# Rearranging the first stage, the way into block two, and the way out of its attention

## The reference

```python
# block one
proj = x @ w_in + b_in                      # 22 tiles of 256 columns; f (the forget gate) first
y_a = hgrn2_mixer(q, f, i, g) @ w_proj_a    # chunked linear attention, 4 heads
y_b = moba_mixer(mq, mk, mv) @ w_proj_b     # softmax attention, 8 heads of 64
mixed = (sigmoid(gate_a) * y_a + sigmoid(gate_b) * y_b) @ w_out
x = layer_norm(ALPHA * x + mixed)
x = layer_norm(ALPHA * x + hier_moe(x))     # 32 experts, top 2
# block two, on 16 meta tokens + 256 tokens (L = 272)
h = concat(meta, x)
h = h + pool_mixer(rmsnorm(h), pool_w)      # windows 2, 4, 8, 16; then 4 blocks of 256x256
h = h + swiglu(rmsnorm(h), gate, up, down)  # 1024 -> 2816 -> 1024
h = h + sb_mixer(rmsnorm(h))                # stick-breaking attention, 16 heads
h = h + swiglu(rmsnorm(h), gate, up, down)
out = rmsnorm(h)[16:]
```

## Time and profile before

| what | us |
|---|---|
| median of 3 runs | 1244.81 (1243.44 to 1244.97) |
| the profiled execution: its own time | 1242.74 |
| its span | 1241.4 |
| TensorE matmul busy | 1095.2 (88%) |
| VectorE / ScalarE / GpSimd busy | 584.9 / 476.6 / 96.9 |
| mean granted TensorE clock | 0.946 of full |
| DMA | 329.84 MB, 266 GB/s on average |
| chain that ended last | PE 59%, DMA 31%, VectorE 3% |

### The profile page before, as it was taken

How to read it: one execution, slowest core, us unless ns; L and a number is a source line. 1 busy time by engine, 2 the same in 40 slices (tenths; PEclk the granted TensorE clock), 3 DMA queues, 4 the chain that set the end, 5 groups by cost and what they waited for, 6 DMA issues and landing times.

```text
span 1241.4 us, 22394 instructions
## 1 busy us (share of the span) xinstructions
PE 1095.2 (88%) x9774; PEld 913.4 (74%) x9774; DVE 584.9 (47%) x859; ACT 476.6 (38%) x634; POOL 96.9 (8%) x94
## 2 busy tenths in 40 slices
PE   8999999998666767666676999999999998999998
PEld 7999889864232323232333999999999998999997
DVE  5765657633212222212112766664554556666643
ACT  6544763132111111111123644433357764444432
POOL 1540000000000000000000210000110007000011
PEclk9999999999897878888878899999999999999999
DMA  9943547999999999999999746545534245565530
GB/s 336 303 148 116 187 150 300 422 419 420 422 421 420 421 421 421 420 421 420 412 421 403 251 155 201 188 153 171 186 114 142 86 128 178 170 203 164 178 101 35
DMA packets 144689, 329.84 MB, mean 266 GB/s; under 512 B 5507, under 2 KB 115388, under 8 KB 119886
## 3 DMA queue, kind: packets, MB, share of 16 engines
q1 hardware_dynamic: 142528, 321.99, 68.8%
q10 hardware_dynamic: 1470, 4.29, 1.0%
q0 software_dynamic: 592, 2.10, 0.5%
HBM read 327.30 MB, written 1.06 MB: 264 GB/s over the span
## 4 chain that ended last, share of the span: by engine, by line
PE 59%; DMA 31%; DVE 3%; ACT 2%; POOL 2%; issue 2%; SPq 0%; DVEq 0%; ACTq 0%; POOLq 0%
PE PS L444 14%; PE PS L445 14%; PE PS L446 14%; DMA half<-in_w_down_dram 9%; DMA spare<-in_w_down_dram 8%; DMA raw<-in_w_down_dram 7%; DMA half<-in_w_gate_up_dram 5%; PE PS L779 3%; DMA spare<-in_w_gate_up_dram 2%; PE PS L454 1%; PE PS L455 1%; PE PS L456 1%; PE PS L520 1%; PE PS L765 1%; ACT hi L1308 1%
## 5 line engine op out<-in xcount | busy, mean ns | idle before, releaser
L1788 DVE TENSOR_TENSOR lo<-raw,hi 128x2048 fp32r<-128x2048 f32 (+1 forms) x112 | 252.4, 2258 | 143.3 <-ACT hi L1308 112.1
L1308 ACT CAST hi<-raw 128x2048 fp32r<-128x2048 f32 (+1 forms) x113 | 209.5, 1858 | 101.1 <-PE PS L446 90.3
L444 PE MATMUL PS<-AH,hi 128*128 128x272 f32 (+1 forms) x832 | 238.1, 286 | 1.3 <-DVE AL L2273 1.3
L446 PE MATMUL PS<-AH,lo 128*128 128x272 f32 (+1 forms) x832 | 237.6, 286 | 0.0
L445 PE MATMUL PS<-AL,hi 128*128 128x272 f32 (+1 forms) x832 | 237.3, 285 | 0.0
L444 PEld LDWEIGHTS PS<-AH,hi 128*128 128x128 f32 x832 | 157.4, 189 | 2.2 <-issue 1.2
L446 PEld LDWEIGHTS PS<-AH,lo 128*128 128x128 f32 x832 | 157.3, 189 | 0.0
L445 PEld LDWEIGHTS PS<-AL,hi 128*128 128x128 f32 x832 | 156.9, 189 | 0.1
L2204 DVE TENSOR_TENSOR Y<-PS,Y 32x256 fp32r<-32x256 f32 x128 | 53.9, 421 | 131.4 <-ACT Y L1513 128.5
L2195 DVE TENSOR_TENSOR T<-T,PS 64x256 f32<-64x256 f32 x32 | 13.5, 423 | 193.1 <-ACT T L1505 193.0
L445 PE MATMUL PS<-FL,hi 128*128 128x272 f32 (+1 forms) x352 | 100.3, 285 | 0.0
(11 more groups left out here) (402 smaller groups left out, 1952.0 us busy)
## 6 DMA issues: line engine op xcount, KB each, us to landing
raw<-in_w_gate_up_dram SPq DMA_DIRECT2D x45, 1024.0 KB, 27.0
spare<-in_w_gate_up_dram SPq DMA_DIRECT2D x43, 1024.0 KB, 27.0
half<-in_w_gate_up_dram SPq DMA_DIRECT2D x40, 1024.0 KB, 27.3
half<-in_w_down_dram SPq DMA_DIRECT2D x23, 1024.0 KB, 27.0
raw<-in_ffn_w_gate_dram SPq DMA_DIRECT2D x22, 1024.0 KB, 5.2
raw<-in_ffn_w_up_dram SPq DMA_DIRECT2D x22, 1024.0 KB, 5.6
raw<-in_w_in_dram SPq DMA_DIRECT2D x21, 1024.0 KB, 9.8
raw<-in_w_down_dram SPq DMA_DIRECT2D x21, 1024.0 KB, 27.5
```

The source lines that it names most:

```text
L444: pe.matmul(o, w(h, c), xh(k), start=start and c == c0, stop=False)
L446: r = pe.matmul(o, w(l, c), xh(k), start=False, stop=stop and c == c0 + len(ks) - 1)
L1308: act.copy(K.view(K.hi[i % HN], 0, [[1, n]]), K.view(K.rbuf[i], 0, [[1, n]])).then_inc(S.hi, 1)
L1788: r = e.tensor_tensor(K.view(K.lo[i % HN], 0, [[1, n]]), K.view(K.rbuf[i], 0, [[1, n]]), K.view(K.hi[i % HN], 0, [[1, n]]).bitcast(F32), A ...
```

## The change

1. **Unit 1 direct.** The second half of the f projection is multiplied in float32, as the first is; its `hi` and `lo` go.
2. **Rests inside the softmax.** `dve_ahead(17 + g)` stands behind the negation, where VectorE waits for the exponentials, instead of at the head of the step.
3. **Banks of the output projections swapped.** Units 22 and 24 use banks 2 and 3, units 23 and 25 banks 0 and 1; unit 22 waits for unit 20's evacuation, unit 23 for unit 21's.
4. **Into block two.** `first_means` moves in front of the last expert's third up tile; seven matmuls without use (`fill`) are put behind the last downs; `first_pools` becomes eight products with 32 rows, four side by side (`first_units`), and two transposes; `first_pools` and `mix(0, 0)` move in the order; `mix(0, 0)` waits for the first of layer norm's two operations only; the squares are taken in halves as soon as each is there; two of the eight pool weight scalings go from VectorE to GpSimd.
5. **First up tile of feed-forward one direct.** Its `hi` and `lo` go, and ScalarE makes a third, float32 copy of each normalized chunk (`XF`).
6. **Rests back on VectorE.** The two rests that GpSimd made go to VectorE, one between the halves of `wo(3)`, one behind the last chunk; ScalarE rounds the second tile in quarters between chunks; the second feed-forward's first gate tile runs chunk by chunk.

```diff
@@ memory
-    K.direct = [0, *range(E0, P0 + 1)]
+    K.direct = [0, 1, *range(E0, P0 + 1), P0 + 2]
@@ pe_mixers, first
+        loaded(pe, K, S, 1)
+        for k in range(8):
+            for m in range(2):
+                r = pe.matmul(bank(1, 256 * m, [1, 256]), view(K.rbuf[1], 256 * k + 128 * m, [[1, 128]]), view(K.xraw, 256 * k, [[1, 256]]),
+                              start=k == 0 and m == 0, stop=k == 7, skip_group_check=True)
+        r.then_inc(S.unit, 1)
...
-            i, b = 22 + 2 * w + j, 2 * j
+            i, b = 22 + 2 * w + j, 2 * (1 - j)
             if w == 0 and j == 0:
                 pe.wait_ge(S.hg_dve, 6)
-                bank_left(pe, K, S, 21)
-            elif w == 0:
                 bank_left(pe, K, S, 20)
                 pe.wait_ge(S.mo_sl, 4)
+            elif w == 0:
+                bank_left(pe, K, S, 21)
@@ pe_experts
+            if e == NE - 1 and j == 2:
+                first_means()
...
-    def first_pools():
+    def first_units():
         pe.wait_ge(S.um, 2)
+        pe.wait_ge(S.pwn, 6)
+        pe.wait_ge(S.pwn_pool, 2)
+        for c in range(2):
+            for g in range(4):
+                r = pe.matmul(bank(PB, 0, [1, 256], p0=32 * g, rows=32), view(K.MW, 2 * NMETA * (2 * g + c), [[1, 2 * NMETA]]),
+                              view(K.PW, 256 * (2 * g + c), [[1, 256]]), start=c == 0, stop=c == 1)
         r.then_inc(S.um_pe, 1)
+    def fill(n):
+        for _ in range(n):
+            pe.matmul(bank(GB + 1, 0, [1, 256]), con("ident"), view(K.cm, 0, [[1, 256]]), start=True, stop=True)
...
         elif e == NE - 1:
-            first_means()
+            pe.wait_ge(S.ht, NE)
+            fill(4)
     if e1 == NE:
         down(NE - 1)
+        fill(3)
         last_combine()
-        first_pools()
+        first_units()
@@ pe_second
+    def first_pools():
+        pe.wait_ge(S.um, 3)
+        for m in range(2):
+            r = pe.transpose(bank(PB, 256 + 128 * m, [1, 128]), view(K.MU, 128 * m, [[1, 128]]), con("ident"))
+        r.then_inc(S.um_pe, 1)
     turn(0, 0)
+    first_pools()
     turn(0, 1)
     units(0, 0)
     units(0, 1)
     turn(1, 0)
+    mix(0, 0)
     turn(1, 1)
-    mix(0, 0)
     units(1, 0)
@@ mix
-            pe.wait_ge(S.x1_dve, 6)
+            pe.wait_ge(S.x1_mid, 4)
@@ pe_ffn, f == 0 and i == 0, for each k
+                pe.wait_ge(S.xf, k + 1)
+                for m in range(2):
+                    r = pe.matmul(bank(b(1, m), 0, [1, w]), view(K.rbuf[units[1]], 256 * k + 128 * m, [[1, 128]]), tc(K.XF, k),
+                                  start=k == 0, stop=k == 7)
@@ act_second
+    for n in range(2):
+        round_part(act, K, S, K.P0 + 1, n, 4)
     act.wait_ge(S.um_pe, 2)
-    act.copy(K.MM[:, :], bank(PB, 0, [1, 16 * NMETA])).then_inc(S.um, 1)
-    round_half(act, K, S, K.P0 + 1, 0)
+    act.copy(K.MU[:, :], bank(PB, 0, [1, 256])).then_inc(S.um, 1)
     turned(0, 0)
-    round_half(act, K, S, K.P0 + 1, 1)
+    act.wait_ge(S.um_pe, 3)
+    act.copy(K.MM[:, :], bank(PB, 256, [1, 256])).then_inc(S.um, 1)
+    round_part(act, K, S, K.P0 + 1, 2, 4)
     turned(0, 1)
-    act.wait_ge(S.x1_dve, 4)
-    act_squares(act, K, S, 2, rows(0))
+    act_half_squares(act, K, S, 0, 0)
     act_sqrt_row(act, K, S, 1, 4)
+    act_half_squares(act, K, S, 0, 1)
+    round_part(act, K, S, K.P0 + 1, 3, 4)
     act_root(act, K, S, 2)
...
         act_chunk(act, K, S, 0, k, par("nf", k), 0)
+        act.activation(view(K.XF, L * k, [[1, L]]), hc(K.HH, k), ACT.Copy, scale=par("nf", k)).then_inc(S.xf, 1)
@@ dve_mixers, moba_softmax(g)
         dve.tensor_scalar(sm(68, 4), sm(64, 4), -1.0, None, ALU.mult).then_inc(S.mo_neg, 1)
+        dve_ahead(dve, K, S, 17 + g, K.E0)
         dve.wait_ge(S.mo_exp, g + 1)
...
     for g in range(4):
-        project(18 + g)
+        if g == 3:
+            dve_ahead(dve, K, S, 21, K.E0)
@@ dve_attention
-    for m in range(2):
-        wo(3, m)
+    wo(3, 0)
+    rest_lo(dve, K, S, K.at["fg", (1, 0)])
+    wo(3, 1)
...
     dve_chunk(dve, K, S, 2, 7, par("nf", 15), NMETA)
+    rest_lo(dve, K, S, K.at["fu", (1, 0)])
```

More of the change, by code:

```diff
@@ L402, in memory @@
     K.hi_at = {i: n + 1 for n, i in enumerate(K.split)}
[L404 to L406 removed]
+    K.lo_at = K.hi_at
     K.pj = {0: ("a0", 2), 1: ("a0", 4)}
@@ L528, in pe_mixers @@
     first()
-    for u in range(1, 4):
+    for u in range(2, 4):
         project(u)
@@ L956, in units @@
             pe.wait_ge(S.y_lo, 4 * NE)
-            pe.wait_ge(S.um, 3)
+            if h:
+                pe.wait_ge(S.um, 4)
         for g in (2 * h, 2 * h + 1):
@@ L1054, in pe_ffn @@
         if f == 0 and i == 0:
-            for n in units:
-                lo_done(pe, K, S, n)
+            lo_done(pe, K, S, units[0])
+            loaded(pe, K, S, units[1])
             for k in range(8):
                 normed(k)
-                for which in range(2):
+                pe.wait_ge(S.xf, k + 1)
+                for m in range(2):
+                    if k == 0:
+                        bank_free(f, b(0, m))
+                    r = stationary(pe, K, units[0], bank(b(0, m), 0, [1, w]), m, (k,), xh, xl, start=k == 0, stop=k == 7, c0=k)
+                if k == 7:
+                    r.then_inc(S.unit, 1)
+                for m in range(2):
+                    if k == 0:
+                        bank_free(f, b(1, m))
+                    r = pe.matmul(bank(b(1, m), 0, [1, w]), view(K.rbuf[units[1]], 256 * k + 128 * m, [[1, 128]]), tc(K.XF, k),
+                                  start=k == 0, stop=k == 7)
+                if k == 7:
+                    r.then_inc(S.unit, 1)
+            continue
+        for which, n in enumerate(units):
+            lo_done(pe, K, S, n)
+            if f == 0 and which == 0:
+                for k in range(8):
+                    normed(k)
                     for m in range(2):
@@ L1063, in pe_ffn @@
                             bank_free(f, b(which, m))
-                        r = stationary(pe, K, units[which], bank(b(which, m), 0, [1, w]), m, (k,), xh, xl, start=k == 0, stop=k == 7, c0=k)
-                    if k == 7:
-                        r.then_inc(S.unit, 1)
-            continue
-        for which, n in enumerate(units):
-            lo_done(pe, K, S, n)
+                        r = stationary(pe, K, n, bank(b(which, m), 0, [1, w]), m, (k,), xh, xl, start=k == 0, stop=k == 7, c0=k)
+                r.then_inc(S.unit, 1)
+                continue
             for m in range(2):
@@ L1075, in pe_ffn @@
                     pe.wait_ge(S.rs_dve, 6 if i else 1)
-                r = stationary(pe, K, n, bank(b(which, m), 0, [1, w]), m, range(8), xh, xl, before=normed if f == 0 and which == 0 and m == 0 else None)
+                r = stationary(pe, K, n, bank(b(which, m), 0, [1, w]), m, range(8), xh, xl)
             r.then_inc(S.unit, 1)
@@ L2280, in factor @@
     def factor(n):
-        dve_rms_factor(dve, S, own, n, *(K.sm(80 + 2 * n + c) for c in range(2)))
+        dve_rms_factor(dve, S, own, n, *(K.sm(80 + 2 * n + c) for c in range(2)), other=K.sm(105))
     def norm(i, between=None):
```

116 lines of the change are left out of this document (50 added, 66 removed).

## The result

The changed kernel takes **1230.33 us** (median of 4; 1228.47 to 1232.08), beside 1244.12 for the kernel before (median of 4; 1241.1 to 1244.97). The ratio is 0.9893, with a 95% interval of 0.987 to 0.9916: 13.8 us faster, where 11.2 were forecast. A second series on another occasion gave 1230.49 beside 1243.09. The profiled execution of the changed kernel took 1232.08, the slowest of its four; its span is 1230.5 (before: 1241.4).

A forecast was written before the change was run, and what follows sets the result against it. DMA was taken to bound the expert stage and TensorE, with four places of waiting, the rest. Terms 0.4 - 1.1 - 3.6 - 3.9 + 1.2 - 4.2 = -11.2 took the median 1244.8 to 1233.6 us, range 1229.5 to 1238.5.

The forecast's parts named there:

- The slower rival: Block two: the clock stays at the lower level through mixes and the first double tile, giving 1259 us; chance 0.03.
- Unit 1 direct, +0.4: Start: direct float32 matmuls take 1.1 us more than split ones, less a 0.66 us wait for the rest; 0.4 us slower.
- Rests inside the softmax, -1.1: Softmax attention: rests moved into VectorE's wait for the exponentials remove all but 0.2 of TensorE's 1.3 us of waits.
- Banks swapped, -3.6: Unit 22: the 2.17 us wait for unit 21's evacuation goes, and 1.4 us of lower clock behind it.
- Passing the expert stage: Expert stage: DMA's restart and the stream's end move with TensorE, so all 4.3 us of the first stage's gain pass.
- The rival of the swallowed gain: Expert stage: a load, not TensorE, sets DMA's restart at 208 us; only 6.9 us remain, giving 1237.9; chance 0.08.
- Into block two, -3.9: Last combine to first feed-forward matmul: 4.5 us earlier at full clock, less 0.6 for a possible lower-clock stretch.
- The rival of the clock that stays low: Into block two: lower clock through half of 13.0 us loses 3.3 to 6.5 us more, middle 1238.5; chance 0.12.
- Up tile direct, +1.2: Block two's first feed-forward: the direct up tile costs 0.15 us more per chunk, eight times; ScalarE's copies stay hidden.
- Out of attention, -4.2: In `wo(4)`: the 3.27 us wait and 1.4 us of lower clock go, against about 0.5 us of new wait.
- the third rival: End: VectorE's rests or GpSimd's squares come late; 1.5 us come back, or 3 with the clock, 1235.1 to 1236.6; chance 0.15.
- not doing what it says: Unit 22 and `wo(4)`: waits taken for gone are replaced by others, leaving 1241.4 us; chance 0.04.

The follow-up runs named there:

- run 8: The run 4 kernel with unit 1 split again instead of direct: 1229.64 us.
- runs 9 and 10: The run 8 kernel with five and with six idle products ahead of unit 0 in place of four: 1230.21 us and 1229.19 us.
- runs 1 and 2: The changed kernel with VectorE's rests back at the head of each softmax step, and with the banks of units 22 to 25 as before: 1231.66 and 1231.42 us.
- run 6: The changed kernel with the pooled meta rows made as before, by 32 matmuls of 32 columns without transposes, in the new place: 1233.28 us.
- run 7: The run 4 kernel with the first up tile of block two's first feed-forward split again: 1228.24 us.
- run 5: The changed kernel without the seven matmuls of fill ahead of the last combine: 1231.18 us.
- run 3: The changed kernel with the rests of the last feed-forward's first two tiles back on GpSimd, rounding and gate tile as before: 1231.67 us.
- run 4: The changed kernel with VectorE's rest of the last feed-forward's fourth tile made to wait for GpSimd's squares: 1227.96 us, 1227.87 when repeated.

## Why the prediction was right, and where its steps were not

The forecast of 1233.6 in a range of 1229.5 to 1238.5 held 1230.33, and each of the four places changed as named. But of its terms the rests' and the banks' were mis-sized, unit 1's has the other sign in half of the traces, and the late squares were missing.

That the sum came out is in good part luck. In the table above the traces differ by 10.94 where 11.2 were forecast, but only because two misses cancel: the softmax stage, the way in and the way out gave 2.8 more than forecast, and the wait and the clock behind the late squares took 3.2 back, which the sum had at nothing. The range held by luck too. Its working names two ends, 0.6 of clock and 0.2 left of the 1.3, which lead from 1233.6 to 1232.8, and 1.5 of scatter leads to 1231.3; 1231.5 and 1229.5 don't follow from them, and the measured 1230.33 lies below 1231.3. (The slower rival's sum is 1259.9, not 1259. And the page has TensorE at nine tenths or more in slices 2 to 9 and 23 to 39 but for slice 34, not from 21 on; this changes no term.)

- **Unit 1 direct, +0.4.** The traced execution gave +0.28, and run 8 0.5: right for that execution. Wrong as a term for the median. I priced it from a start in which unit 0 took 8.90 us, called that a cold start, and did not ask what happens in an execution that starts warm. There the split unit waits for VectorE and the direct one does not, and the term is -1.6. With four idle products ahead, unit 0 took 7.1 us in 6 of 12 traces. The kernel before keeps nothing of that, the changed one all of it, 2.05 us from its one trace to the other. This is the likeliest source of what the medians gained (13.8 and 12.6 in the two series) beyond the 10.9 of the two first traces, both of which began with a slow unit 0. It is argued, not shown: of the kernel before there is no trace with a quick one, only runs 9 and 10, which have its unit 1. And unit 0 is not all that varies: in runs 8 to 10, where the split unit 1 hides it, the four executions still lie 1.8 to 2.7 us apart.
- **Rests inside the softmax, -1.1.** Measured 2.2 with the new banks, and 4.8 alone. The step that failed is "of the 1.3 us": I took the sum of a waits row as the price. Start to start the same waits were 1.96, and the transposes behind such a wait took up to 0.06 longer each time (0.88 against 0.82).
- **Banks swapped, -3.6.** Measured 3.9 alone, so idle 2.17 and clock 1.4 were well read for that case. But on top of the rests it is only 1.24. Together 6.05 for a forecast of 4.7. That two parts share one wait and one clock stretch I had not considered.
- **Passing the expert stage.** Right. The stage took 502.68 before and 502.54 after. In the other traces it took up to 504.04, whatever the kernel; differences of a us or so in single traces mean nothing there. The rival of the swallowed gain is refuted by runs 1 and 2 as well.
- **Into block two, -3.9.** Measured -4.82. Laid out step by step it was 4.5 less 0.6 for a possible clock stretch; the stretch did not come. It stayed away in both traces of the changed kernel. The small products themselves are 1.1 of the 4.82 (run 6), where the forecast's layout made them the main thing, the direct up tile, which spares ScalarE and VectorE a tile there, is 1.28 (run 7), and the idle matmuls are 0.3 of it (run 5). The other 2.1 lie in what no run took back by itself: the order, the halved squares, GpSimd's scalings, or what the parts share. The rival of the clock that stays low was not put to the test. In run 5 the lower level did come, at a cost of 1.2, but it ended at the second set of transposes, where the rival had it last through half of the 13.0 us; its 3.3 to 6.5 are neither borne out nor refuted. The Trainium skill (TensorE: Matmul & The Clock Gate, Part 1) makes the throttled state the default that activity releases; run 5 agrees, with a granted clock of 0.55 from 676 to 684 us without the seven idle matmuls and 1.00 in the same stretch with them.
- **Up tile direct, +1.2.** Measured +1.28 in its tile, and -1.28 ahead of it, which the forecast did not credit.
- **Out of attention, -4.2.** The idle time and the clock went as priced, -4.70. The term itself was wrong, because it stopped there: the third rival, "GpSimd's squares for the sum behind it", came true beside it, with 1.73 of wait and 1.50 of clock, the upper of its two prices of 1.5 and 3. Net the term is 1.5 (run 3), not 4.2. I gave the rival 0.15; that its time of 1236.6 did not come as well is owed to what the other places gave beyond their terms. That TensorE waits for GpSimd's squares behind `wo(4)` also stood among the signs of being wrong. The profile had the evidence. In the earlier trace rows an instruction of 0.50 took 4.80 beside GpSimd's rest, and the other side of the same collision stood in the same trace of before, a square of GpSimd and a rest of VectorE (the two timelines at 1048 us):

```profile
1048.28 2.48 POOL L2564 TENSOR_TENSOR SQ<-HH 128x256 f32<-128x256 f32 x1
```

```profile
1047.98 2.30 DVE L1788 TENSOR_TENSOR lo<-raw,hi 128x2048 fp32r<-128x2048 f32 x1 [1.13 <-ACT hi L1308]
```

  Two such squares left a wait of 0.6 there; a third rest and an earlier need had to make it longer. The Trainium skill (GPSIMD Engine Reference, the table at its head) was quoted for just this. By it I should have made it a term and not a rival; run 4 settles it for the third rest, with 2.48 beside it and 0.62 without.
- **Slower, and not doing what it says:** neither happened.

## What to carry to other kernels

Price a wait of a pipelined engine from start to start against its cadence, not by the idle column. When work moves from a slow engine to a fast one whose instructions hold the slow one up, price both sides: list what the slow engine still does beside the moved work, and who waits for it. Parts of a change that touch the same wait are not to be added; a two by two of runs shows what they share.
